# One embedding stage moved beside the last rows, and the last group's chain packed more tightly beside the rows of the group before

## The reference

```
z   = rmsnorm(x) @ w_in                       # 2048 x 7176
mix = [retention heads, mLSTM heads](z) @ w_out   # recurrent states run over blocks of frames
h   = x + mix
c   = rmsnorm(h);  q = c @ w_peer_q           # 8 heads of 256
per head: top 16 of 128 keys on each half, top 16 of their pairs -> 128 experts per frame, gate = softmax
h  += sum_k gelu(c . u[expert_k]) * gate_k * v[expert_k]      # u, v: 16384 x 2048
h  += sigmoid(rmsnorm(h) @ w_ple_gate) * (p @ w_ple_proj)
y   = rmsnorm(h)
```

## Time and profile before

| | |
|---|---|
| median of 3 runs | 4576.89 us (4567.49 to 4578.49) |
| profiled execution | 4562.5 us, its span 4560.7 us |
| PE, DVE, ACT, POOL busy | 2240.6, 3148.2, 386.1, 2245.9 us |
| bytes moved | 1588.88 MB |
| last row of v ends | 4392.6 us |

### The profile page before, as it was taken

How to read it: one execution, slowest core, us unless ns; L and a number is a source line. 1 busy time by engine, 2 the same in 40 slices (tenths; PEclk the granted TensorE clock), 3 DMA queues, 4 the chain that set the end, 5 groups by cost and what they waited for, 6 DMA issues and landing times.

```text
span 4560.7 us, 20194 instructions
## 1 busy us (share of the span) xinstructions
PE 2240.6 (49%) x6644; PEld 1223.2 (27%) x6644; DVE 3148.2 (69%) x3367; ACT 386.1 (8%) x863; POOL 2245.9 (49%) x1156
## 2 busy tenths in 40 slices
PE   7975888865765064767674373550047000000047
PEld 3445433343354023222233231550023000000023
DVE  0015564545689858777777957899967899999951
ACT  1021000022010001000002200000010000000001
POOL 0000474523554336722324745765646788878830
PEclk9987899986977586898987686775569555555578
DMA  8853898967997589999998989996789999999975
GB/s 251 288 203 134 341 396 338 383 241 286 389 381 279 221 350 385 414 413 413 414 413 326 393 324 415 417 415 263 306 345 410 416 422 422 422 401 422 422 291 172
DMA packets 362432, 1588.88 MB, mean 348 GB/s; under 512 B 36632, under 2 KB 42520, under 8 KB 211608
## 3 DMA queue, kind: packets, MB, share of 16 engines
q0 software_dynamic: 165888, 1208.03, 65.4%
q1 hardware_dynamic: 195064, 369.60, 23.0%
q10 hardware_dynamic: 1376, 9.96, 0.6%
HBM read 1578.58 MB, written 8.92 MB: 348 GB/s over the span
## 4 chain that ended last, share of the span: by engine, by line
DMA 30%; PE 27%; POOL 18%; DVE 16%; issue 7%; ACT 2%; SPq 0%; DVEq 0%; POOLq 0%; ACTq 0%
PE psum L530 21%; DMA W<-in_w_in 16%; POOL ring L478 9%; POOL ring L474 9%; DVE arena L1421 5%; DMA ring<-in_peer_v,eidx 4%; DMA ring<-in_peer_u,eidx 4%; DVE ring L1408 3%; PE psum L704 3%; DMA W<-in_w_out 3%; DMA W<-in_w_ple_gate 2%; DVE arena L1307 1%; DMA W<-in_w_peer_q 1%; PE psum L567 1%; DVE actT L508 1%
## 5 line engine op out<-in xcount | busy, mean ns | idle before, releaser
L530 PE MATMUL psum<-W,actT 128*128 128x512 f32 x3520 | 1659.6, 632 | 362.1 <-DMA W<-in_w_in 237.1
L478 POOL DMA_INDIRECT ring<-in_peer_v,eidx x576 | 1180.2, 2049 | 1183.3 <-DVE arena L1421 989.7
L474 POOL DMA_INDIRECT ring<-in_peer_u,eidx x576 | 1065.5, 1850 | 953.4 <-DVE gate L1323 448.1
L1421 DVE SCALAR_TENSOR_TENSOR arena<-ring,wts,arena 128x2048 f32<-128x2048 f32 x576 | 1353.0, 2349 | 189.6 <-DMA ring<-in_peer_v,eidx 170.0
L1408 DVE CUSTOM_DVE_ANT_0 ring<-ring,cx 128x2048 f32<-128x2048 f32 x576 | 1316.6, 2288 | 180.6 <-DMA ring<-in_peer_u,eidx 162.7
L530 PEld LDWEIGHTS psum<-W,actT 128*128 128x128 f32 x3520 | 704.8, 203 | 1305.1 <-issue 924.3
L517 PE MATMUL psum<-misc,arena 128*128 128x128 f32 x240 | 54.5, 421 | 1617.8 <-ACT arena L491 1605.9
L517 PEld LDWEIGHTS psum<-misc,arena 128*128 128x128 f32 x240 | 49.0, 227 | 1625.0 <-issue 1485.7
L704 PE MATMUL psum<-actT,W 128*128 128x128 f32 (+2 forms) x1536 | 276.6, 345 | 55.5 <-DMA W<-in_w_peer_q 34.6
L704 PEld LDWEIGHTS psum<-actT,W 128*128 128x128 f32 x1536 | 256.7, 203 | 74.4 <-DMA W<-in_w_peer_q 37.4
L1355 DVE TENSOR_TENSOR arena<-psum,arena 128x512 f32<-128x512 f32 x20 | 13.8, 690 | 221.4 <-PE psum L756 219.2
(11 more groups left out here) (188 smaller groups left out, 1302.7 us busy)
## 6 DMA issues: line engine op xcount, KB each, us to landing
W<-in_w_in SPq DMA_DIRECT2D x168, 1024.0 KB, 20.4
W<-in_w_ple_gate SPq DMA_DIRECT2D x64, 1024.0 KB, 11.1
W<-in_w_out SPq DMA_DIRECT2D x48, 1024.0 KB, 13.5
W<-in_w_peer_q SPq DMA_DIRECT2D x48, 1024.0 KB, 16.9
ring<-in_peer_u,eidx POOLq DMA_INDIRECT x576, 16.4
ring<-in_peer_v,eidx POOLq DMA_INDIRECT x576, 16.3
arena<-in_x_prompt SPq DMA_DIRECT2D x8, 1024.0 KB, 6.6
cx<-in_g_ffn ACTq DMA_DIRECT2D x5, 1024.0 KB, 8.8
```

The source lines that it names most:

```text
L474: pool.indirect_dma_start(ring[:, x % 4, :], None, a["peer_u"][0], off(ix, 0)).then_inc(u_in[x % 4], 16)
L478: pool.indirect_dma_start(ring[:, 4 + x % 4, :], None, a["peer_v"][0], off(ix, 0)).then_inc(v_in[x % 4], 16)
L530: ins = pe.matmul(bank(4 * s + j), aT(k, j), W[:, k, :], start=(k == 0), stop=(k == KT - 1))
L1421: dve.scalar_tensor_tensor(out=hslot(t), in0=ring[:, 4 + slot, :], scalar=wts[:, n % DEEP, c:c + 1], in1=hslot(t), op0=ALU.mult, op1=ALU.a ...
```

## The change

Two constants, and the place of one embedding in ACT's and DVE's queues. PE's, SP's and POOL's programs are untouched.

```
-CHAIN_AT = {0: (0, 0), 1: (0, 0.95), 2: (18, 1.7)}
-EMBED_AT = {0: (0, 1), 1: (0, 1.3), 2: (0, 0), 3: (0, 0)}
+CHAIN_AT = {0: (0, 0), 1: (0, 0.95), 2: (18, 1.0)}
+EMBED_AT = {0: (0, 1), 1: (0, 3.5), 2: (ROWS[3] + LAG + 2, 2.5), 3: (0, 0)}
```

In shadow_act (and in the same way in shadow_dve):

```
             else:
                 yield from act_embed(act, 1)
+                yield embed_step(2, 0)
+                yield from act_embed(act, 2)
```

More of the change, by code:

```diff
@@ L1009, in scalar @@
                 act_gather(act, grp, Beside(shadow_act(act, g)))
-            Beside(act_embed(act, 2)).finish()
             Beside(act_embed(act, 3)).finish()
@@ L1384, in shadow_dve @@
                 yield from dve_embed(dve, 1)
+                yield embed_step(2, 0)
+                yield from dve_embed(dve, 2)
         def dve_gather(dve, grp, side):
@@ L1430, in vector @@
                 dve_gather(dve, grp, Beside(shadow_dve(dve, g)))
-            Beside(dve_embed(dve, 2)).finish()
             Beside(dve_embed(dve, 3)).finish()
```

## The result

The changed kernel takes 4603.88 us (median of 7 runs, 4590.36 to 4614.74) against 4574.61 us (7 runs, 4564.15 to 4578.49): ratio 1.0063, 95% interval 1.0043 to 1.0082, so 20 to 38 us slower. Forecast was +57 us. The direction and the mechanism were right, the forecast size was twice the measured one.

The account below looks back on a forecast made before the run. DMA, with 416 GB/s as full rate, was taken to bound the kernel wherever the ring of gathered rows is kept going. Terms 102 - 12 + 44 - 77 = +57 us on 4576.9 gave 4634 us, range 4560 to 4690.

Parts of the forecast that it names:

- Term 1: Chain 2 beside group 1's rows, at 1.0 instead of 1.7: 102 us more unfilled time, from 49 to 159.
- rival A: Whole kernel: bytes alone decide, full buffers refill in the chain's short stops, chain edit free; -45, 4532 us; chance 0.12.
- The two additions in the upper bound: Chain 2: late start, up to 27 us, and state exchange between blocks 3 and SB, up to 30 us.
- The exchange of states: Between blocks 3 and SB, through SP: 45 us from first store to first load, adding up to 30 us.
- The late start: Start of chain 2: its gate product ends 59 us after row 18, adding up to 27 us.
- Term 2: Embedding 1 beside group 2's first rows, at 3.5 instead of 1.3: its waits go, -12 us, from -19 to 0.
- Terms 3 and 4: Embedding 2 moved beside rows, +44 us (40 to 80); tail with embedding 3 alone, -77 us (-71 to -80).
- Term 3: Embedding 2 beside rows: +44 us for bytes and sharing; DVE's work and late products hidden, uncovered +12 and +36.
- The reading of the queues: Gather and weights' queues alternate packets; weights get 89 GB/s, 7.3 rows a column group, so tighter placement stops rows.
- B: Whole kernel: no change, the chain's price at its lower end of 49 us; +4, 4581 us; chance 0.12.
- C: Whole kernel: worse, late start and states in full, chain's price 159 us; +114, 4691 us; chance 0.12.
- D: Embedding 2 falls behind the rows, losing its lead or staying partly in the tail: +36, 4670 us; chance 0.11.

Follow-up runs that it names:

- E5: The changed kernel with group 2's chain at 1.35 rows a unit instead of 1.0: 4540.26 us, ratio 0.9931 to the kernel before.
- E4: The changed kernel with group 2's chain at 0.95 rows a unit instead of 1.0: 4627.96 us, ratio 1.0118 to the kernel before.
- E8: The changed kernel with state n stored and loaded in 16-byte pieces as it lies, its transposition left out: 4587.78 us, ratio 1.0038 to the kernel before.
- E3: The kernel before with only embedding 1 changed, to 3.5 rows a unit instead of 1.3: 4551.09 us, ratio 0.9954.
- E2: The changed kernel with group 2's chain back at 1.7 rows a unit, both embedding edits kept: 4525.23 us, ratio 0.9898 to the kernel before.
- E12: E2 with embedding 2 at 1.2 rows a unit instead of 2.5: 4539.87 us, ratio 0.9926 to the kernel before.
- E1: The kernel before with only group 2's chain changed, to 1.0 rows a unit instead of 1.7: 4637.63 us, ratio 1.0135.

## Why the prediction was wrong in size

Term 1, chain 2 at 1.0: forecast 102 us in a range of 49 to 159; measured 69 us in the trace, 62 alone and 76 beside the embeddings by runs. This is the step that failed, and in it the words "Between the two measured placements: 110 x (1.7 - 1.0) / (1.7 - 0.95)". A straight line was laid through two points of a curve with a knee (E5, E4): 15 us at 1.35 where a line gives about 48. The end of the line was good: E4, chain 2 at chain 1's scale, costs 101 us by runs and 80 + 77 + 17 + 17 + 63 = 254 us unfilled against chain 1's 248. The fact from which the knee follows stood in the text, in rival A, as the 20 us in which eight buffers fill; I used it to dismiss A and not to shape the curve. If stops shorter than that cost little, the price need not be a line in the pace. Its stages were off too: scores and picks were to bear 27 of the 110, but the picks have 60 to 66 us unfilled in every version whose windows were taken, bound by DVE's own work (99 of 102 us busy in the changed kernel); the product with w_in bears 50 of the 66. And the long stop before w_out's products, which the prediction read as the chain's one stop at 1.7, is paid at either pace.

The two additions in the upper bound hardly show. The exchange of states took 24.5 us from first store to first load in the changed kernel instead of 45; the DMA engines moved 320 GB/s in that stretch, against 398 in the same stretch of the kernel before, and whether that is the reason is not shown. E8 puts what 9 of these us cost at some 10 us, and does not tell it from nothing. The late start shows as stops of 9.4, 13.7 and 31.2 us in its first 18 rows; the longest ran at 409 GB/s for its first 25 us.

Term 2, embedding 1: forecast -12, trace -12 (19 to 6 us unfilled), E3 -21 (-29 to -13). Right by the trace; by runs just outside the stated -19 to 0.

Terms 3 and 4 together: forecast -33; E2 less E3 gives -26. The tail took 96.3 us instead of 91: the copy of the fold and the norm came sooner as said, but the fold itself took 6.66 us for the 3.67 before, and the first column group still took 15.28 us though its weights had landed (no DMA moved in the 15 us from 4500 us on). So the 1.6 us for that were not there, and the prediction's reason for the 15.52 us was wrong. The window of the first column group, before and then in the changed kernel, has a granted clock of 0.90 and 0.91, behind stretches at 0.50 and 0.56 in which PE worked 4.3 of 7.7 us and 6.5 of 15 us; the next group's 13.73 us have 1.00, the 2.4 GHz level, in both:

```profile
4484.76:4500.28 15.52, 15.52 (x33) 6.99 (x34) 0.00 (x0) 1.25 (x1) 0.00 (x0) 0.90 0.77 261
4512.85:4528.13 15.28, 15.28 (x33) 6.84 (x34) 0.00 (x0) 1.25 (x1) 0.00 (x0) 0.91 0.54 180
```

Term 3's hidden parts were hidden: 418 GB/s in rows 136 to 184, and with half its rows taken away (E12) the stops for late products come, 37.9 us of them, at a price of some 13 us that its runs do not set apart from the noise.

The reading of the queues held: the stops at the waits that group 0 had named, bare rows at 421 GB/s, group 2's first row late by the unfilled time (69 us late, 66 us unfilled). Rival A needed less than 45 us and is excluded by E1; B's +4 is outside the interval; C's +114 and D's +93 did not come. That the median of 4604 us still fell into the stated range is no merit of term 1: the range was wide.

## What to carry to other kernels

When work is woven beside a stream that keeps a ring of buffers full, price each stop as its length less what the ring still takes in (some 25 us for 8.4 MB in the product with w_in, less or nothing at other waits, as the windows show), not as a line in the pace. Find the few long waits, those that stand at every pace too, and give rows to just those places: the version with 1.55 and room at two waits beats an even 1.7 that ends at the same row by 31 us. And moving an embedding that stood bare behind the last row brought a good third of its time here (26 of 72 us), when its bytes have to come beside rows that already fill the DMA engines.

## What the runs showed of the hardware that I had not expected

The fold at the start of the tail, 8 matmuls of 128x512, took 3.67 us before, where PE had just run embedding 2 (granted clock 1.00, the 2.4 GHz level, in that window), and 6.64 us in the changed kernel, where PE had idled for 130.7 us; the granted clock in the window was 0.55, near the 1.2 GHz level.

```profile
4492.40:4499.00 6.60, 6.59 (x8) 2.50 (x8) 0.00 (x0) 0.00 (x0) 0.00 (x0) 0.55 0.00 0
```

So moving work of PE away from the tail makes the first work left there dearer, by 3 us here. *Trainium skill, "TensorE: Matmul & The Clock Gate", section "What's actually happening": the array is clocked down after idling and up after work; this trace agrees, 6.64 against 3.67 us.*
